# Decay products amid the latent key tiles, head 0's decay alone, and output gate chunks 2 and 3 in the first head of the chunked-attention ring

## What is computed

```python
log_a = log_sigmoid(ga @ alpha_w + alpha_b) / 16          # 4 heads x 128, per token
# GLA, per head, in chunks: b = cumsum(log_a)
scores = einsum('td,sd,tsd->ts', q, k, exp(b[t] - b[s]))  # s <= t
o = rms_norm(scores @ v + exp(b) q @ state) * silu(gr)    # gr: the output gate, 1024 wide
c_kv = rms_norm_2(dkv, ckv_g)                             # latent key, 128 wide
```

## Time and profile before

| | us |
|---|---|
| runs shown (3): median, lowest, highest | 2201.43, 2199.3, 2204.84 |
| the profiled execution: time | 2204.3 |
| the profiled execution: span | 2202.4 |
| TensorE busy in the span | 2158.6 |
| VectorE, ScalarE, GpSimd busy | 992.6, 753.0, 1005.0 |
| mean granted TensorE clock | 0.993 |

### The profile page before, as it was taken

One profiled execution on the slowest core, in us unless ns is written; L12 is line 12 of the kernel. 1 busy time (PEld: TensorE's weight loads), 2 busy tenths in 40 slices (PEclk: granted clock), 3 DMA queues, 4 the chain that ended last, 5 costly groups with the idle time before them and its releaser, 6 DMA issues.

```text
span 2202.4 us, 31272 instructions
## 1 busy us (share of the span) xinstructions
PE 2158.6 (98%) x12472; PEld 1855.5 (84%) x12472; DVE 992.6 (45%) x1451; ACT 753.0 (34%) x1003; POOL 1005.0 (46%) x812
## 2 busy tenths in 40 slices
PE   8999999989999999999999999999999999999998
PEld 7897999989999887888888777878777888888886
DVE  5244454279888208322201618671875452322017
ACT  4133455343222216222213324552336332222134
POOL 4322223455555547555544543254331555555444
PEclk9999999999999999999999998999999999999999
DMA  4321111212222323222222221024220223222222
GB/s 163 101 73 63 58 59 58 97 58 96 95 95 82 113 100 113 99 95 97 93 105 93 104 90 56 20 77 137 93 77 20 83 91 111 90 103 96 95 97 95
DMA packets 31837, 194.94 MB, mean 89 GB/s; under 512 B 3968, under 2 KB 4480, under 8 KB 9984
## 3 DMA queue, kind: packets, MB, share of 16 engines
q1 hardware_dynamic: 26352, 182.66, 23.3%
q10 hardware_dynamic: 5392, 10.95, 1.5%
HBM read 189.24 MB, written 4.23 MB: 88 GB/s over the span
## 4 chain that ended last, share of the span: by engine, by line
PE 82%; issue 7%; DVE 5%; POOL 4%; ACT 1%; DMA 0%; SPq 0%; DVEq 0%; POOLq 0%; ACTq 0%
PE ps L2207 72%; POOL wlo L664 4%; PE ps L2757 2%; PE ps L2865 1%; DVE sqa L1437 1%; PE ps L2892 1%; PE ps L2975 1%; PE ps L2949 1%; DVE x2lo L1425 1%; ACT whi L727 1%; PE ps L2486 0%; PE ps L2509 0%; PE ps L2930 0%; PE ps L2545 0%; DMA h<-h 0%
## 5 line engine op out<-in xcount | busy, mean ns | idle before, releaser
L664 POOL TENSOR_TENSOR wlo<-raw,whi 128x512 fp32r<-128x512 f32 (+2 forms) x808 | 1004.8, 1275 | 1174.1 <-ACT whi L727 1078.1
L727 ACT CAST whi<-raw 128x2048 fp32r<-128x2048 f32 x165 | 315.2, 1910 | 822.0 <-PE ps L2207 764.3
L2207 PE MATMUL ps<-x2hi,whi 128*128 128x512 f32 x1136 | 450.1, 396 | 1.2 <-DVE x2lo L1425 1.1
L2207 PE MATMUL ps<-x2hi,wlo 128*128 128x512 f32 x1136 | 443.6, 391 | 0.0
L2207 PE MATMUL ps<-x2lo,whi 128*128 128x512 f32 x1136 | 443.5, 390 | 0.0
L2207 PE MATMUL ps<-xhi,whi 128*128 128x256 f32 x1344 | 276.5, 287 | 21.4 <-DVE xlo L1490 9.6
L2207 PE MATMUL ps<-xlo,whi 128*128 128x256 f32 x1344 | 273.4, 285 | 0.0
L2207 PE MATMUL ps<-xhi,wlo 128*128 128x256 f32 x1344 | 273.2, 285 | 0.0
L2207 PEld LDWEIGHTS ps<-x2hi,whi 128*128 128x128 f32 x1136 | 214.1, 188 | 50.1 <-issue 5.3
L2207 PEld LDWEIGHTS ps<-x2hi,wlo 128*128 128x128 f32 x1136 | 214.1, 188 | 45.1
L2207 PEld LDWEIGHTS ps<-x2lo,whi 128*128 128x128 f32 x1136 | 214.2, 189 | 44.0 <-issue 1.4
(11 more groups left out here) (442 smaller groups left out, 2741.1 us busy)
## 6 DMA issues: line engine op xcount, KB each, us to landing
raw<-wstream SPq DMA_DIRECT2D x170, 1024.0 KB, 4.8
h<-h SPq DMA_DIRECT2D x4, 528.0 KB, 8.5
ncb<-c_rows ACTq DMA_DIRECT2D x8, 256.0 KB, 3.5
ple_rows<-ple_out ACTq DMA_DIRECT2D x4, 512.0 KB, 4.0
bias<-bias_rows ACTq DMA_DIRECT2D x8, 256.0 KB, 4.5
ple<-ple_rows ACTq DMA_DIRECT2D x4, 512.0 KB, 5.4
out_dram<-outb SPq DMA_DIRECT2D x8, 256.0 KB, 2.8
raw<-wstream ACTq DMA_DIRECT2D x4, 256.0 KB, 7.3
```

What stands on the lines that cost most here:

```text
L664: return nc.gpsimd.tensor_tensor(wlo[b][:, cols], raw[b][:, cols], whi[b][:, cols].bitcast(F32), ALU.subtract)
L727: nc.scalar.copy(whi[b][:], raw[b][:]).then_inc(sig("hi_done"), 1)
L2207: ins = mm(dst, w[slot][:, cols], xx(tok), start=first and p_ == 0, stop=last and p_ == 2, skip_group_check=True)
```

## The change

- The four transposes of `iw` and the four low-rank products go into the middle of `U_SPC`'s last chunk, after its fourth tile, and write banks 5, 6, 7 and 1 in place of 4 to 7. The latent key's sum of squares goes to bank 4.
- Head 0's decay goes through VectorE and ScalarE alone; the other three heads' add, minimum, Exp and Ln follow, their `ramp` stands in turn 1 of the ring, their sum in turn 4, and the scans of heads 1, 2 and 3 in turns 5, 14 and 23. Each scan has its own `negs`, and `nb_ready` counts heads. The refinement of the latent key's root and `ckvf` go to turn 3, the copy of its transposes to turn 7, the transposes to TensorE's turn 6.
- Tiles 16 to 31 (gate chunks 2 and 3) go into the ring. `GR_IN_STEP` says how many tiles each turn has: 20, 9, 8 and 11 in the four heads, three in each of q = 2 to 6, none in q = 13, 14, 22, 23 and 31.
- ScalarE's casts follow: the second gate unit ahead of the squares, the third in turns 1 and 2, the fourth in turns 9 to 12, the unit behind the gates in turns 22, 23, 24 and 26. Gate chunks are copied out in the turn after the one that completes them.
- `ax`, `restart`, `negs` and one `gf` buffer move to other addresses, so that the decay of later heads lives beside the ring's buffers.

```diff
@@ -367,13 +367,13 @@
...
         kx2 = at("kx2", [P, 2, P], offset=arena + 89088)
-        ax = at("ax", [P, 4, SEQ], offset=temp)
+        ax = at("ax", [P, 4, SEQ], offset=arena + 40960)
         al = at("al", [P, 4, SEQ], offset=arena + 32768)
-        restart = at("restart", [P, SEQ], offset=x_spare)
-        gf = [at(f"gf{i}", [P, SEQ], offset=(temp, temp + 2048, x_spare)[i]) for i in range(3)]
+        restart = at("restart", [P, SEQ], offset=arena + 81920)
+        gf = [at(f"gf{i}", [P, SEQ], offset=(temp, temp + 2048, arena + 83968)[i]) for i in range(3)]
         sd = [at(f"sd{i}", [P, 4, P], offset=temp + 4096 + 5120 * i) for i in range(2)]
         sx = [at(f"sx{i}", [P, 6, P], offset=temp + 6144 + 5120 * i) for i in range(2)]
-        negs = at("negs", [P, 4, 8], offset=x_spare + 2048)
+        negs = at("negs", [P, 4, 8], offset=temp + 14784)
         g1s = at("g1s", [P, 4, SEQ], offset=arena + 65536)
...
@@ -584,10 +584,22 @@
...
 
+        GR_IN_STEP = (1, 3, 3, 3, 3, 3, 1, 1, 2, 2, 1, 1, 0, 0, 1, 1, 1, 2, 1, 1, 1, 0, 0, 1, 1, 1, 2, 1, 1, 1, 0,
+                      1, 1, 2, 2, 2)
+        assert len(GR_IN_STEP) == NG and sum(GR_IN_STEP) == 3 * UT
+
         def gr_tiles_by(q):
 
-            i, part = (q - 1) // 9, (q - 1) % 9
-            return 8 * i + (0, 0, 1, 2, 3, 4, 5, 6, 8)[part]
+            return UT + sum(GR_IN_STEP[:q])
+
+        def gr_chunks_after(q):
+
+            last = gr_tiles_by(q - 1) if q else UT - 1
+            return [c for c in range(1, 8) if last < KC * (c + 1) <= gr_tiles_by(q)]
+
+        def alpha_bank(hd):
+
+            return bank((5, 6, 7, 1)[hd])
 
...
@@ -1132,32 +1144,32 @@
...
             act.dma_start(scratch.ap(), brow[:]).then_inc(sig("brow_out"), 16)
-            for u in range(U_GV, U_GR):
+            for u in range(U_GV, U_GR - 1):
                 hi_of(u + 2)
-
+            nc.scalar.preload_act_table_set("natural_log_exp_and_others")
+
+            def decay(part, heads):
+
+                act.wait_ge(sig("decay_x"), part)
+                step.up(nc.scalar.activation(al[:, heads], al[:, heads], ACT.Exp))
+                step.wait()
+                nc.scalar.activation(al[:, heads], al[:, heads], ACT.Ln, bias=one_col).then_inc(sig("decay_ln"), 1)
+
+            act.wait_ge(sig("brow_out"), 16)
+            decay(1, slice(0, 1))
+            hi_of(U_GR + 1)
             act.wait_ge(sig("evac2"), U_GR - U_GQK)
-            nc.scalar.preload_act_table_set("natural_log_exp_and_others")
             nc.scalar.activation(sq[0][:, 0:SEQ], dkvf[:], ACT.Square).then_inc(sig("ckv_sq"), 1)
+            decay(2, slice(1, 4))
             act.wait_ge(sig("ckv_sums"), 1)
-            rsqrt_of(bank(1), 1.0 / P)
+            rsqrt_of(bank(4), 1.0 / P)
             gr_out(0)
 
-            act.wait_ge(sig("decay_x"), 1)
-            act.wait_ge(sig("brow_out"), 16)
-            step.up(nc.scalar.activation(al[:], al[:], ACT.Exp))
-            step.wait()
-            nc.scalar.activation(al[:], al[:], ACT.Ln, bias=one_col).then_inc(sig("decay_ln"), 1)
-
-            gr_out(1)
-            act.wait_ge(sig("ckv_ready"), 1)
-            act.dma_start(ik_low[64:P], narrow[0:64]).then_inc(sig("ik_in"), 16)
-            gr_out(2)
-            gr_out(3, False)
             for q in range(NG + 4):
...
                     hd, kind = GI[q]
-                    if q == 7:
-                        act.wait_ge(sig("nb_ready"), 1)
+                    if kind == 7:
+                        act.wait_ge(sig("nb_ready"), hd + 1)
                     if kind == 8:
...
@@ -1183,12 +1195,19 @@
...
                         nc.scalar.activation(gf[q % 3][:], gf[q % 3][:], ACT.Exp).then_inc(sig("g_e"), 1)
-                if q % 9 == 1 and q > 1:
-                    gr_out(q // 9 + 3, False)
-                if 1 <= q <= 4:
-                    hi_quarter(U_GR + 3, q - 1)
-                if 20 <= q <= 23:
-                    hi_quarter(U_MG1, q - 20)
+                if 1 <= q <= NG + 1:
+                    for c in gr_chunks_after(q - 1):
+                        gr_out(c, False)
+                if q in (1, 2):
+                    hi_quarter(U_GR + 2, 2 * q - 2)
+                    hi_quarter(U_GR + 2, 2 * q - 1)
+                if q == 5:
+                    act.wait_ge(sig("ckv_ready"), 1)
+                    act.dma_start(ik_low[64:P], narrow[0:64]).then_inc(sig("ik_in"), 16)
+                if 9 <= q <= 12:
+                    hi_quarter(U_GR + 3, q - 9)
+                if q in (22, 23, 24, 26):
+                    hi_quarter(U_MG1, min(q - 22, 3))
                 m = q - 2
...
@@ -1941,40 +1960,69 @@
...
             vec.tensor_copy(narrow[0:GA.stop], bank(5)[0:GA.stop]).then_inc(sig("narrow_out"), 1)
-            dve.wait_ge(sig("unit_done"), U_SPC + 1)
-            vec.tensor_copy(dkvf[:], bank(4)).then_inc(sig("evac2"), 1)
-            for hd in range(4):
-                dve.wait_ge(sig("alpha_done"), hd + 1)
-                step.up(vec.tensor_scalar(ax[:, hd, :], bank(4 + hd), cv[:, C_AB + hd:C_AB + hd + 1], None, ALU.add))
-            step.wait()
-            vec.scalar_tensor_tensor(out=al[:], in0=ax[:], scalar=-1.0, in1=ax[:], op0=ALU.mult, op1=ALU.min
-                                     ).then_inc(sig("decay_x"), 1)
-            scale = refined(bank(1), 1.0 / P)
-            dve.wait_ge(sig("evac2"), U_GR - U_GQK)
-            vec.scalar_tensor_tensor(out=ckvf[:], in0=dkvf[:], scalar=cv[:, C_CKV:C_CKV + 1], in1=scale,
-                                     op0=ALU.mult, op1=ALU.mult).then_inc(sig("ckv_ready"), 1)
-            dve.wait_ge(sig("decay_x"), 1)
-            step.up(vec.tensor_scalar(ax[:], ax[:], -1.0 / 16, 0.0, ALU.mult, ALU.max))
             step.up(vec.memset(restart[:], 1.0))
...
             step.up(vec.memset(restart[:].rearrange("p (j c) -> p j c", c=P)[:, :, 0:1], 0.0))
-            dve.wait_ge(sig("decay_ln"), 1)
-            step.up(vec.scalar_tensor_tensor(out=ax[:], in0=al[:], scalar=1.0 / 16, in1=ax[:],
-                                             op0=ALU.mult, op1=ALU.add))
-            step.wait()
-            for hd in range(4):
-                if hd == 3:
+
+            def decay_in(heads):
+
+                for hd in range(heads.start, heads.stop):
+                    dve.wait_ge(sig("alpha_done"), hd + 1)
+                    step.up(vec.tensor_scalar(ax[:, hd, :], alpha_bank(hd), cv[:, C_AB + hd:C_AB + hd + 1], None,
+                                              ALU.add))
+                step.wait()
+                vec.scalar_tensor_tensor(out=al[:, heads], in0=ax[:, heads], scalar=-1.0, in1=ax[:, heads],
+                                         op0=ALU.mult, op1=ALU.min).then_inc(sig("decay_x"), 1)
+
+            def decay_ramp(heads, part):
+
+                dve.wait_ge(sig("decay_x"), part)
+                step.up(vec.tensor_scalar(ax[:, heads], ax[:, heads], -1.0 / 16, 0.0, ALU.mult, ALU.max))
+
+            def decay_out(heads, part):
+
+                dve.wait_ge(sig("decay_ln"), part)
+                step.wait()
+                step.up(vec.scalar_tensor_tensor(out=ax[:, heads], in0=al[:, heads], scalar=1.0 / 16,
+                                                 in1=ax[:, heads], op0=ALU.mult, op1=ALU.add))
+
+            def decay_sum(hd):
+
+                step.wait()
+                step.up(vec.tensor_tensor_scan(nbt[:, hd, :], restart[:], ax[:, hd, :], 0.0, ALU.mult, ALU.add))
+                step.wait()
+                ends = nbt[:, hd, :].rearrange("p (j c) -> p j c", c=P // 2)[:, :, P // 2 - 1:]
+                vec.tensor_scalar(negs[:, hd, :].rearrange("p (j a) -> p j a", a=1), ends, -1.0, None, ALU.mult
+                                  ).then_inc(sig("nb_ready"), 1)
+
+            head0, others = slice(0, 1), slice(1, 4)
+            decay_in(head0)
+            decay_in(others)
+            dve.wait_ge(sig("unit_done"), U_SPC + 1)
+            vec.tensor_copy(dkvf[:], bank(4)).then_inc(sig("evac2"), 1)
+            decay_ramp(head0, 1)
+            decay_out(head0, 1)
+            decay_sum(0)
+            vec.tensor_scalar(iwt, bank(0)[:, 0:32], float(np.float32(8 ** -0.5)), None, ALU.mult
+                              ).then_inc(sig("iw_ready"), 1)
+
+            for q in range(NG + 2):
+                if q == 1:
+                    decay_ramp(others, 2)
+                if q == 3:
+                    scale = refined(bank(4), 1.0 / P)
+                    dve.wait_ge(sig("evac2"), U_GR - U_GQK)
+                    vec.scalar_tensor_tensor(out=ckvf[:], in0=dkvf[:], scalar=cv[:, C_CKV:C_CKV + 1], in1=scale,
+                                             op0=ALU.mult, op1=ALU.mult).then_inc(sig("ckv_ready"), 1)
+                if q == 4:
+                    decay_out(others, 2)
+                if q == 5:
+                    decay_sum(1)
+                if q == 7:
                     dve.wait_ge(sig("ckv_turned"), 1)
```

(47 more changed lines are left out.)

## The result

The changed kernel takes 2211.96 us (median of 6, 2209.92 to 2213.68), the kernel before beside it 2202.28 (median of 6, 2198.87 to 2204.84). The ratio is 1.0048, 95% interval 1.0038 to 1.0058: slower by 9.7 us, where 2204.4 and a range of 2195 to 2210 had been forecast. One thing is needed to read the numbers of this kernel: executions of the kernel before differ by whether the clock falls in the ring. Of the 88 taken beside the experiments, 44 took 2198.5 to 2200.3 us (median 2199.3, mean clock mostly 0.995 or 0.996), 37 took 2202.8 to 2205.1 (median 2203.4, clock 0.992 to 0.993), 7 lay between. The lower level is the same on every chip used, but the share above 2200.5 us ran from 3 of 13 to 19 of 29, so a median of this kernel depends on how many of its executions have the fall.

What follows compares the result with a forecast made beforehand. TensorE, busy 98%, was taken as the bound. Gaps +7.7 and the old fall -8.2 gave -0.5; a new fall +3.5 made +3.0 us, taking the median from 2201.4 to 2204.4, range 2195 to 2210.

Steps and rivals of the forecast that it cites:

- Steps 1 to 3: Up to the ring's start: low-rank move free, item 0's products at 1327.9, old waits of 0.8 and 2.66 us gone.
- Cost 0: Low-rank products inside the latent unit's second half: their input is ready before the fourth tile, so no time is added.
- Steps 4 and 5: Head 0: VectorE's added queue work and GpSimd's SBUF reads delay item 2's factors, gap between 0.6 and 4.7 us.
- the upper bound: Gap ahead of item 2: 4.7 us taken, with four GpSimd pieces blocking four VectorE operations by 1.0 us each.
- Step 6: Scans at q = 14 and 23, queued behind a waiting copy: gaps of 3.7 us in head 1, 2.7 in head 2.
- The sum of the gaps: TensorE's gaps over all four heads: 14.0 us against 6.3 before, so +7.7 us.
- Step 7: Clock in the ring: one new fall, ahead of item 2 or 13, costing 3.5 us (2.1 to 4.5).
- The old fall: Clock fall early in the old ring: its slow TensorE turns lose 8.2 us, credited as -8.2 if removed.
- The last line of the sum: Profiled execution to median: 2204.3 becomes 2207.3 us, and the median 2201.4 becomes 2204.4.
- the clock is low through output products: Rival, 18%: a fall at item 13 lasting to q = 20 doubles 4.44 us of output products, 2208 to 2212 us.
- Clock stays up: Rival, 20%: same gaps in the ring but none brings the clock down, 2200.9 us.

Runs made afterwards that it cites:

- e4: Kernel before with only the low-rank block moved into the latent unit and all heads' decay together ahead of the ring: 2198.44 us, ratio 0.9989.
- e1: Changed kernel with 18, 12 and 9 idle products in the gaps ahead of items 2, 13 and 22: 2203.99 us, ratio 1.0006.
- e11: Changed kernel with GpSimd's work on the third gate unit's low half in 16 pieces of 128 columns, not 4 of 512: 2209.60 us, ratio 1.0042.
- e2: Changed kernel with the scans of heads 2 and 3 one step earlier on VectorE, ahead of the waiting copy: 2206.99 us, ratio 1.0023.
- e8: Kernel before with nine idle products in its old 2.66 us wait ahead of item 1: 2198.88 us, ratio 0.9990.
- e3: Changed kernel with the latent key's root refinement and normalisation one turn earlier on VectorE: 2208.45 us, ratio 1.0030.
- e9: Kernel before with the low-rank block moved into the latent unit and four idle products ahead of item 1: 2198.54 us, ratio 0.9990.

## Why the prediction was wrong

Its walk through the queues held. Its count of falls did not, and that is the step that failed. A second error, from the profiled execution to the median, is about as large.

- *Steps 1 to 3.* Item 0's products: 1327.98 against 1327.9. No wait ahead of item 1. The low-rank block, "Cost 0", cost nothing in the profiled execution of the changed kernel, whose clock stayed up there. That the clock can fall at it was not foreseen: in e4 a fall of 3.4 us cost 1.6 us of TensorE's time, in e1 one of 6.8 us cost 3.2. Whether the other five executions of the changed kernel had one is not known.
- *Steps 4 and 5.* Gap ahead of item 2 4.51 against 4.7, from four operations held 1.0 us each, as written; e11 shows the cause. That the upper bound was taken was right.
- *Step 6.* 3.43 and 2.46 against 3.7 and 2.7. e2 confirms the scan behind the waiting copy: without it 2.12 and 1.19.
- *The sum of the gaps.* 11.1 us in five waits against 14.0. The small ones had been put at 2.9 us, and only 0.7 came. The term was +7.7 and measured 11.1 - 6.3 = +4.8, so this error alone would have made the forecast 2.9 us too high.
- *Step 7, the one that failed:* "I take one fall in the ring, ahead of item 2 or 13", at 3.5 us. There were three, one at each of the three long gaps, worth 7.6 us by the rows of e1 and 8.0 by its median. The term was 3.5, so it was 4.1 us too small, the largest error in the walk. The price of one fall, 3.5, was too high (2.3 to 3.0 measured); the count was what failed. The step argued from the old fall that the new gaps "look like the first kind", and then counted one of them. By its own argument each of the three long gaps was a candidate.
- *The old fall.* It was credited at 8.2 us, by TensorE's turns alone. In the kernel before it is worth 4.1 to 5.7 (e8 and the executions without it), since VectorE is next in line in the same turns. That the trace agreed with half of the throttled time holds for TensorE's own turns (8.2 against 8.5), not for what the fall is worth. In the changed kernel, whose turns in head 0 have three tiles, it can't be measured apart: 5.6 = 4.8 + 7.6 - 6.8, so 6.8 us are left for it and for all that was priced at nothing.
- *The last line of the sum*, from the profiled execution to the median. The forecast put the changed kernel's profiled execution at 2207.3 and its median 2.9 us under it, because the profiled execution of before stands 2.9 above its median. It came out the other way: the profiled execution took 2209.92 and the median is 2.0 above it. Of the 7.6 us by which the forecast missed, 2.6 are in the profiled execution and 4.9 in this line. Only some executions of the kernel before have the old fall, so its median already holds part of the fall's absence; the forecast took the fall for all of them.

A sum of the profiled executions that does not use the medians starts from e8, the kernel before without its fall, span 2196.8. The gaps add 3.9 (11.1 against 7.2 in e8's ring, fillers counted as waiting) and the three falls 7.6, which makes 2208.3; the changed kernel's span is 2208.0. The prediction had -0.5 without falls against a kernel with one, and +3.5. By its own prices three falls would have made +10.0, or 2211.4, close to the measured 2211.96; that would have been luck, since the gaps, the price of a fall and the last line were off in both directions.

Of the rivals, "the clock is low through output products" named 2208 to 2212, but for another reason: the fall at item 13 lasted 6.8 us, not over 12. Its time was right by luck (the measured 2211.96 is just inside) and its mechanism was not. "Clock stays up" was refuted, and with fillers in the gaps, where it holds in the ring, the time is 2204.0 and not 2200.9; e1's fall at the low-rank block is part of that.

## What to carry to other kernels

When work is moved so that TensorE's few large gaps become several middle ones, price each gap twice: its idle time, and a fall of the clock of its own (here 2.3 to 3.0 us each for gaps of 2.5 to 4.5 us). A fall is not certain at each, so give the number of falls a range. Price a fall that is removed by the engine that is next in line in that stretch, not by TensorE's halves. Ask of a profiled execution whether it is the common one: its time against the spread of the runs tells, and here that question was worth 4.9 us. And where a gap can't be removed, idle products in it are worth a try: they took 8.0 us off the changed kernel, and from the kernel before the executions of about 2203.4 us.

## What the hardware showed that was not expected

- The kernel before has two times 4.1 us apart, 2199.3 and 2203.4; by the mean clock of each execution, and by one profile of either sort (before and e8), they differ by one fall in the ring. Nine idle products in that gap leave only the first.
- The low-rank block, in which TensorE does not wait, comes with a fall of 3.4 to 10.2 us in the profiles of nine versions, and a fall of 6.8 us there costs 3.2 us. With full products amid it the profile has the longest. Its cause is not settled.
- VectorE's two-input operations of 512 columns take 0.69 us alone; beside GpSimd they take 1.65 us with pieces of 512 columns and 0.83 with pieces of 128, and GpSimd's 2048 columns take 6.36 and 11.98 us. Piece width trades one engine's delay for the other's.
- The length of a fall did not follow the length of the gap: behind 4.51 us it was 6.8 us long in the changed kernel and 3.4 in e2, behind 2.46 us 6.8 and 10.2 (changed kernel, e3).
- The best versions, e4 and e9, are 0.1% under the kernel before, less than the 0.3% that can be told from no change.
